# Constant products on TensorE in its waits ahead of the experts, and the last expert's rows placed by one-hot products

## The reference, cut to what matters

```python
logits = t @ w_router                       # 384 x 8
top_logit, top_e = top_k(logits, 2)
gates = softmax(top_logit)                  # two experts and two gates for each token
out[e] = (silu(x_e @ wg[e]) * (x_e @ wu[e])) @ wd[e]    # D_FF = 2816
y[token] = sum over its two experts of gate * out[row of this token]
x = x + mod_gate * y
```

## Time and profile before

| | us |
|---|---|
| median of three timed runs | 1924.35 |
| the profiled execution, its own time | 1944.56 |
| its span, first to last instruction | 1942.8 |
| TensorE busy in the span | 1843.7 |
| mean granted TensorE clock | 0.981 of full |

### The profile page before, as it was taken

The page is one execution under the profiler, slowest core; times in us unless marked ns, Lnnn a source line. Parts: engine busy times, 40 slices in busy tenths (PEclk is TensorE's granted clock), DMA queues, the critical chain, the costliest instruction groups (busy, mean ns, idle before and its releaser), DMA issues.

```text
span 1942.8 us, 31565 instructions
## 1 busy us (share of the span) xinstructions
PE 1843.7 (95%) x13609; PEld 1284.4 (66%) x13609; DVE 536.8 (28%) x1168; ACT 400.4 (21%) x901; POOL 125.2 (6%) x123
## 2 busy tenths in 40 slices
PE   6999999999999999999989999999998999999994
PEld 3554655879999887554785454568653456878783
DVE  2550336135555102165352000201111111111131
ACT  2221226110001001353222110311122121212120
POOL 0000111000000000000001001110010101020202
PEclk8999999999999999999999999999999999999997
DMA  8632237246542234133266556997689998999993
GB/s 311 236 132 87 87 109 260 86 140 206 175 152 76 96 126 177 51 134 134 80 244 216 200 195 204 392 383 251 228 278 394 384 364 301 365 344 359 345 383 126
DMA packets 234141, 427.93 MB, mean 220 GB/s; under 512 B 17694, under 2 KB 88701, under 8 KB 233678
## 3 DMA queue, kind: packets, MB, share of 16 engines
q1 hardware_dynamic: 218496, 411.65, 60.1%
q0 software_dynamic: 11360, 12.43, 1.9%
q10 hardware_dynamic: 4142, 1.72, 0.3%
HBM read 427.34 MB, written 29.00 MB: 235 GB/s over the span
## 4 chain that ended last, share of the span: by engine, by line
PE 88%; DMA 5%; DVE 3%; issue 2%; SPq 1%; ACT 1%; POOL 0%; POOLq 0%; DVEq 0%; ACTq 0%
PE bank L1099 24%; PE bank L588 11%; PE bank L824 10%; PE bank L1227 6%; PE bank L1192 6%; PE bank L876 6%; PE bank L635 4%; PE bank L1130 2%; PE bank L700 2%; PE bank L494 2%; DMA ring<-in_moe_w_gate_dram 2%; DMA ring<-in_w_mod_dram 1%; PE bank L919 1%; PE bank L908 1%; PE bank L552 1%
## 5 line engine op out<-in xcount | busy, mean ns | idle before, releaser
L1099 PE MATMUL bank<-ring,HTXN 128*32 128x384 f32 (+3 forms) x3104 | 287.6, 393 | 6.0 <-issue 3.9
L1318 ACT ACTIVATE arena<-bank 128x512 f32<-128x512 f32 (+3 forms) x317 | 140.8, 507 | 588.7 <-PE bank L824 178.6
L1099 PEld LDWEIGHTS bank<-ring,HTXN 128*32 128x32 f32 (+2 forms) x3104 | 202.9, 120 | 84.1 <-issue 61.1
L1099 PE MATMUL bank<-arena,HTXN 128*32 128x384 f32 (+3 forms) x2336 | 224.4, 394 | 2.6 <-issue 1.6
L1099 PEld LDWEIGHTS bank<-arena,HTXN 128*32 128x32 f32 (+2 forms) x2336 | 157.4, 122 | 63.3 <-issue 44.8
L2274 DVE TENSOR_TENSOR arena<-arena,bank 128x512 f32<-128x512 f32 x120 | 76.7, 683 | 414.3 <-PE bank L1099 385.2
L588 PE MATMUL bank<-ring,HTXN 128*128 128x512 f32 (+4 forms) x528 | 153.0, 452 | 1.0 <-DVE HTXN L2105 1.0
L1663 ACT ACTIVATE arena<-bank 128x512 f32<-128x512 f32 x120 | 65.0, 597 | 372.8 <-PE bank L1099 325.4
L588 PEld LDWEIGHTS bank<-ring,HTXN 128*128 128x128 f32 x528 | 96.2, 190 | 57.1 <-issue 47.2
L824 PE MATMUL bank<-HTXN,arena 128*128 128x192 f32 x704 | 121.4, 326 | 0.0
L876 PE MATMUL bank<-ring,arena 128*128 128x256 f32 x528 | 114.2, 379 | 2.6 <-DVE arena L2032 2.6
(11 more groups left out here) (349 smaller groups left out, 1849.0 us busy)
## 6 DMA issues: line engine op xcount, KB each, us to landing
ring<-in_moe_w_up_dram SPq DMA_DIRECT2D x53, 1024.0 KB
ring<-in_moe_w_gate_dram SPq DMA_DIRECT2D x49, 1024.0 KB
ring<-in_w_mod_dram SPq DMA_DIRECT2D x24, 2048.0 KB, 9.3
ring<-in_moe_w_down_dram SPq DMA_DIRECT2D x48, 1024.0 KB
arena<-in_moe_w_down_dram SPq DMA_DIRECT2D x40, 1024.0 KB
arena<-in_moe_w_gate_dram SPq DMA_DIRECT2D x39, 1024.0 KB
arena<-in_moe_w_up_dram SPq DMA_DIRECT2D x35, 1024.0 KB
ring<-in_w_in_dram SPq DMA_DIRECT2D x10, 2048.0 KB, 11.6
```

The source lines that it names most:

```text
L1099: last = mm(bank[row:row + rows_, col:col + cn], xe[:, i, k, at:at + rows_], wt[:, c0:c0 + cn], start=(k == 0 and col == 0), stop=(k == KT ...
L1318: return act_fn(out, in_, ACT.Copy)
```

## The change

Part one. A helper runs `n` products of the identity with 256 constant columns into a bank that the next real work overwrites. It is called in nine places directly ahead of a wait; in a tenth, twelve products with 128 columns go into unused columns of a bank. Where `fill` stood behind the wait it is moved ahead of it.

Part two. The last turn is kept to widths of up to 128 rows (its bodies for wider experts are gone), and if at least four experts other than expert 0 have more than 128 tokens, two places of the order are exchanged. The last turn writes nothing to DRAM. VectorE makes a table `slots` (token x row, holding the gate where the row is the token's), TensorE transposes it during the output products (`slot_tables`, at the fifth of eleven weight chunks), and after the drain of `yt` TensorE multiplies table by rows (`rows_to_tokens`) into six banks, which VectorE gates and adds to `X`. The late rows of the earlier experts are added during the last turn.

```diff
+            def keep_awake(bank, n):
+                for _ in range(n):
+                    mm(bank[:, 0:2 * P], ident, CST[:, 0:2 * P], start=True, stop=True)
-            def blocks(label, sources):
+            def blocks(label, sources, ready=None, n=0):
                 bank, full = fill(label)
+                if ready is not None:
+                    keep_awake(bank, n)
+                    pe.wait_ge(*ready)
...
-            mod_rows(0, 2)
+            mod_rows(0, 2, n=7)
             first_rows(0)
             mod_columns(0, 2)
+            begun = [fill(("xbc", m, "p")) for m in range(4)]
...
+            keep_awake(begun[0][0], 7)
             for t in range(NT):
                 pe.wait_ge(*drained(("nt", 0, t, 0)))
...
+                for _ in range(12 if j == 0 else 0):
+                    mm(begun[0][0][:, TOK:TOK + P], ident, CST[:, 0:P], start=False, stop=False)
                 for t in range(NT if j == 0 else 0):
                     pe.wait_ge(*drained(("nt", 0, t, 1)))
...
             to_feature_major(1)
+            first_plain = fill(("plain", 0))
+            keep_awake(first_plain[0], 5)
             ht_ready(1)
...
+                blocks(("qaT", t), [...], (qa_ready, t + 1), 5 if t == 0 else 0)
+                    blocks(("hT", i, q), [...], (kq_ready, i + 1) if q == 0 else None, 4 if last_k else 0)
+                blocks(("pT", n), [...], (pr_ready, n + 1), 3 if n == 3 else 0)
...
-            to_feature_major(3)
+            to_feature_major(3, 5)
+            bank, full = fill("lg_lanes")
+            keep_awake(bank, 3)
             ht_ready(3)
...
+            bank, full = fill("rank")
+            keep_awake(bank, 3)
             pe.wait_ge(sel_ready, 1)
...
+            def slot_tables(e, w):
+                pe.wait_ge(slots_ready, 1)
+                for n, label in enumerate(TABLES):
+                    bank, full = moe_fill(label, e)
+                    lanes = range(4) if n == 0 else [3] if w == 96 else []
...
+                    for t in range(NT):
+                        for lane in lanes:
+                            c = 32 * n if w == 96 and lane == 3 else 32 * lane % w
+                            last = mm(bank[32 * lane:32 * lane + 32, t * P:(t + 1) * P], slots[:, t, c:c + 32], ident,
+                                      start=(t == 0), stop=(t == NT - 1))
+                    last.then_inc(full, 1)
+            def rows_to_tokens(e, w):
+                for label in TABLES + [("y", 0, 0), ("y", 0, 1)]:
+                    pe.wait_ge(*moe_drained(label, e))
+                for t in range(NT):
+                    for h in range(2):
...
+                        elif w == 96 and h == 1:
+                            mm(PSUM[b][:, 0:256], table[0][0:96, :], rows_[0:96, 512:768], start=True, stop=False)
+                            for k in range(3):
+                                last = mm(PSUM[b][:, 256:512], table[k][96:P, :], rows_[96:P, 256 * k:256 * k + 256], ...)
+                        else:
+                            last = mm(PSUM[b][:, :], table[0][0:w, :], rows_[0:w, 512 * h:512 * h + 512], ...)
+                        last.then_inc(bank_full[b], 1)
...
-            then(v.tensor_scalar(tmp8, beaten, -2.0, float(2 * NE - 1), ALU.mult, ALU.add))
-            then(v.scalar_tensor_tensor(place_at, beaten, 2.0, tmp8, ALU.mult, ALU.min))
+            v.tensor_scalar(tmp8, ...); v.tensor_scalar(over_128[:, 1:8], cnt[:, 1:8], float(P), None, ALU.is_gt)
+            then(v.tensor_scalar(fourth, ...)); v.scalar_tensor_tensor(place_at, ...)
+            v.scalar_tensor_tensor(fourth, ...); then(v.tensor_reduce(over_128[:, 0:1], ...))
+            then(v.tensor_scalar(over_128[:, 0:1], ...)); then(v.scalar_tensor_tensor(place_at, ...))
...
+                if e == NE - 1:
+                    for t in range(NT):
+                        last = v.tensor_scalar(slots[:, t, :], iota, last_slot[:, t:t + 1], gl[:, t:t + 1], ALU.is_equal, ALU.mult)
+                    last.then_inc(slots_ready, 1)
...
+                else:
+                    moe_copy(TABLES[1], e, slot_t[:, 1, :], ...)
+                    for t in range(NT):
+                        dve.wait_ge(late_loaded[t], 16)
+                        add_rows(late_y, gl_before, t)
...
-            for t in range(NT):
-                dve.wait_ge(late_loaded[t], 32)
-                add_rows(late_y, gl, t)
+            for t in range(NT):
+                for h in range(2):
...
+                    dve.wait_ge(bank_full[b], n)
+                    then(v.tensor_tensor(late_y[:, t, at], PSUM[b][:, :], GB[:, 0 if t == 0 else 1, at], ALU.mult))
+                    v.tensor_tensor(X[:, t, at], X[:, t, at], late_y[:, t, at], ALU.add).then_inc(x_updated, 1)
```

More of the change, by code:

```diff
@@ L515, in ht_ready, with mod_rows @@
                     pe.wait_ge(*drained(("nt", n, t, 1)))
[L517 removed]
+            def mod_rows(layer, j, at=None, n=0):
                 label = ("mod", layer, j)
+                bank, full = fill(("mr", layer, j), at)
+                keep_awake(bank, n)
                 landed(label)
                 w = part(label, KT, 512)
[L523 removed]
                 for k in range(KT):
@@ L939, in _ @@
                         mod_grouped("mla", 1, j)
-                pe.wait_ge(kq_ready, i + 1)
+                last_k = i + 1 < len(TILES) and TILES[i + 1][0] == "k" and all(kind == "q" for kind, _ in TILES[i + 2:])
                 for q in range(2):
-                    blocks(("hT", i, q), [KQN[:, i % 2, 4 * q + k, :] for k in range(4)])
+                    blocks(("hT", i, q), [KQN[:, i % 2, 4 * q + k, :] for k in range(4)],
+                           (kq_ready, i + 1) if q == 0 else None, 4 if last_k else 0)
                 blocks(("hT", i, 2), [kq_v[:, i % 2, D + k * P:D + (k + 1) * P] for k in range(4)])
@@ L1198, in output_96 @@
                 return last
+            def slot_tables(e, w):
[3 more added lines that the diff above has]
+                    lanes = range(4) if n == 0 else [3] if w == 96 else []
+                    if not lanes:
+                        pe.sem_inc(full, 1)
+                        continue
+                    for t in range(NT):
[9 more added lines that the diff above has]
+                    for h in range(2):
+                        b, n = token_bank(t, h)
+                        pe.wait_ge(bank_free[b], n - 1)
+                        table = [slot_t[:, k, t * P:(t + 1) * P] for k in range(3)]
+                        rows_ = yt[:, 0, :]
+                        if w == 64:
+                            last = mm(PSUM[b][:, :], table[0][64 * h:64 * h + 64, :], rows_[64 * h:64 * h + 64, 0:512], start=True, stop=True)
+                        elif w == 96 and h == 1:
+                            mm(PSUM[b][:, 0:256], table[0][0:96, :], rows_[0:96, 512:768], start=True, stop=False)
+                            for k in range(3):
+                                last = mm(PSUM[b][:, 256:512], table[k][96:P, :], rows_[96:P, 256 * k:256 * k + 256], start=False, stop=(k == 2))
+                        else:
+                            last = mm(PSUM[b][:, :], table[0][0:w, :], rows_[0:w, 512 * h:512 * h + 512], start=True, stop=True)
+                        last.then_inc(bank_full[b], 1)
             def output(e, pieces):
@@ L1204, in output @@
                     if q == 2:
-                        for i in range(NPIECE):
+                        for i in range(NPIECE if e + 1 < NE else 1):
                             for h in range(2):
@@ L1270, in _ @@
             ORDER = [2, 1, 0, 3, 4, 5, 6]
-            BODIES = [(e, v) for e in range(NE) for v in ORDER]
+            LAST = NE - 1
+            BODIES = [(e, v) for e in range(NE) for v in ORDER if e < LAST or len(PIECES[v]) == 1]
             pe.br("experts")
@@ L1292, in go_to @@
                 likely = WIDTHS.index(LIKELY[e])
-                order = [likely] + [v for v in ORDER if v != likely]
+                order = [likely] + [v for v in ORDER if v != likely and (e, v) in BODIES]
                 for n, v in enumerate(order[:-1]):
```

87 lines of the change are left out of this document (57 added, 30 removed).

## The result

The changed kernel takes 1914.57 us (median of 8 runs, 1907.51 to 1929.02), the kernel before, on the same chip, 1924.61 (8 runs, 1921.73 to 1927.03). The ratio is 0.9948, 95% interval 0.9927 to 0.9968: 10.0 us faster. Forecast were 24.15 us and a time of 1900.2, with 1912 as the upper end; so the sign was right and less than half of the gain came.

A forecast was written before the change was run, and what follows sets the result against it. TensorE, busy 1843.7 of 1942.8 us, was taken to bound the kernel. Kept clock 17.45 and end less tables 9.5, minus route 0.9 and new falls 1.9, gave 24.15 us: 1924.35 to 1900.2, range 1892 to 1907.

The forecast's parts named there:

- stretches 1 to 3: Low-clock windows at the kernel's start (18.7, 28.9, 52.8); full clock there was to save 8.0 us.
- stretches 7, 8: Low-clock windows at 899.3 (attention) and 998.3; full clock was to save 3.0 and 0.7 us.
- falls that stay or come anew: Anywhere a wait stays open: one low-clock stretch charged at the mean, 1.9 us lost.
- route: VectorE's routing chain ahead of the experts' indices: six more chained operations, 0.9 us lost.
- tables: Last turn: 18 table products of 128 columns amid TensorE's output products, 3.0 us lost, bounds 2.0 to 4.0.
- the end: From last output product to last addition: 10.2 us at full clock instead of 22.7, 12.5 saved.
- rival C: Last products run at 1.2 GHz after the idle 0.8 us: 17.8 instead of 10.2 us, 1907.8 in all; chance 0.08.
- rival B: Products at all ten places run at the lower clock and outlast their waits: 7.7 us slower, 1932.1; chance 0.04.
- stretch 7: Low-clock window in attention (899.3), behind a 1.50 us wait three products were to fill; 3.0 us saved.
- A: At the filled waits, constant products don't hold the clock or only move low stretches: gain 8.6 us, 1915.8; chance 0.08.
- D: In the experts, the weight stream eats the gain won upstream; only the end's is left, 1914.9 us; chance 0.05.
- E: Blocks of 24 transposes count as idle; the clock falls at two places beside them, 1902.5 us; chance 0.08.

The follow-up runs named there:

- part one alone: Kernel before with all the constant products but its own old end; 1919.42 us, ratio 0.9957.
- filled end: Changed kernel plus two constant products in the pause between the last output product and the wait for the drained rows; 1904.78 us, ratio 0.9890.
- front with three: Changed kernel with three instead of seven constant products ahead of the second chunk of modulation weights; 1917.22 us, ratio 0.9952.
- transposes: Kernel with the filled end, each group of n constant products made into 4n transposes, the twelve narrow products kept; 1905.04 us, ratio 0.9887.
- best kernel: Kernel with the filled end, plus five products ahead of the dense block's hidden-rows wait and attention's three moved ahead of their bank's wait; 1902.02 us, ratio 0.9873.
- fill on part two alone: Kernel with only part two, plus two filling products in the pause behind the last output product; 1931.2 us, ratio 0.9939.
- hidden rows' wait filled: Kernel with the filled end, plus five constant products ahead of the wait for the dense block's last hidden tile; 1904.16 us, ratio 0.9879.
- part two alone: Changed kernel without any constant products, keeping the new end, tables and longer route chain; 1926.12 us, ratio 0.9995.
- the last experiment: The best kernel with three instead of seven constant products ahead of the first mod_rows; 1921.11 us, ratio 0.9884.

## Why the prediction was wrong

The steps in the order of its sum. Where a part is seen in a trace with fewer disturbances, I take it from there.

| term | forecast | measured | where |
|---|---|---|---|
| front, stretches 1 to 3 | -8.0 | -4.9 to -5.2 clock up late, -8.2 up early | changed kernel, part one alone; filled end |
| stretch 4 | -1.55 | -1.5 | all |
| stretches 5, 6 | -4.2 | -4.1 | all |
| the wait for a weight chunk behind them | none | 0 to +1.3 by the run, +0.8 in part one alone | all |
| stretches 7, 8 | -3.7 | -0.5 as written with a fall, -2.2 without one, -3.6 with the products in the wait | part one alone; front with three, transposes; best kernel |
| falls that stay or come anew | +1.9 | +3.4 (326 and 647), and others by run | part one alone |
| route | +0.9 | +0.7 | changed kernel against part one alone |
| tables | +3.0 | +2.0 | changed kernel against part one alone |
| waits for code in the last turn | none | +1.8, and -3.0 with the end filled | changed kernel; filled end |
| the end | -12.5 | -5.1 at the lower level, -11.3 held | changed kernel; filled end |

**The step that failed most is the end at full clock**, "10.2 us", and with it rival C, given 0.08. The mechanism was worked out right, and its length nearly: 17.8 forecast for the lower level, 17.66, 17.75 and 16.96 measured in three kernels, 11.5 in every one with the fill. That the 17.8 fits so closely is luck in part: the first tile's products began at full clock and took 3.66 us (1907.98 to 1911.64) instead of 5.2, and the second's took 5.71. What failed was the argument against it, that "the new pause is shorter than any that a fall followed" and the last products stood at full clock. The trace of before had pauses of 1.50 us and longer with a fall, and I took the shortest of them for a bound. Here 1.05 us was enough (priced at 0.8). The fill on part two alone shows that it isn't the falls ahead of the experts. Why so short a pause tips the clock here (behind it stand products of 96 and 32 rows instead of 128) was not separated. At full clock the end is 11.47 and not 10.2 because TensorE is not ahead of VectorE: a tile's products take 2.95 us (1888.17 to 1891.12), not 2.6 at most, the thin ones 0.26 a record and not 0.22. Cost of both: 7.4 us of the missing 14.1, of them 1.3 for the latter.

**The second is the overrun, rival B, at one place.** I had priced it at all ten places together. At the front it was real, 6.14 us of products in a wait of 3.56, since TensorE starts at the lower level; the "0.88 at the lower level" stood in the prediction and wasn't applied where the first `mod_rows` already showed 3.59 us. Cost: 2.9 us. At the other places the products were at full clock and fit, as forecast.

**The third is stretch 7.** The three products were costed as lying in the wait of 1.50 us. But `blocks` issues them behind `fill`, and `fill` itself waits for the bank's drain, which is the late one here (VectorE, `modT`). They came 1.42 us too late and added their own time. In part one alone and with the hidden rows' wait filled the clock fell there all the same (893.3); in three traces with the call at the same place (filled end, front with three, transposes) it didn't, and in two of these stretches 7 and 8 gave 2.2 us. "`fill`, moved ahead of the wait, takes banks that were drained long before" is the sentence that failed; it holds at the other places. Moved ahead of `fill`, they gave 3.6 with stretch 8, as forecast. Cost: 3.2 us with the fall, 1.5 without.

**The fourth is what comes anew.** One stretch was charged; two came in four of the nine traces with part one (326 and 647, which cost 1.7 us each), one of the two in three more, and others by the run. The profiled execution had one of 20.5 us behind the unfilled waits of 1.99 and 0.88 us: ahead of it the kernel was 7.4 us earlier than before, behind it level with it. In the one trace with the wait at 647 filled, another fall stood further on.

**What the sum had at nothing without a word** are the waits for code in the last turn. The one near its start grew from 2.03 to 4.62 us, the one at the up products shrank from 2.23 to 1.43: 1.8 us, and in the profiled run a low stretch of 6.8 us at the first of them besides. The wait at `L1072`, which was to grow to 1.8 us by the route, shrank from 0.90 to 0.16: TensorE now waits 2.23 us at `L1129` (1020.74) instead.

Against these, the tables cost 2.0 us and not 3.0, as much as the lower bound.

Part one alone gained 8.3 us and part two alone 1.0 by their ratios, together 9.3; the changed kernel gained 10.0 (interval 6.2 to 14.0). So there is no sign that one part hinders the other. A closer sum isn't to be had, since the low stretches differ from run to run by more than that: up to the first experts' product the changed kernel and the one with the filled end issue the same work, and their traces have it at 1020.74 and 1008.68.

Of the rivals, A fell (seven places of nine held, and part one alone has a ratio of 0.9957); D fell, by the last experiment's 16.5 and 17.6 us. E fell: the places beside blocks of transposes gave their 1.5 and 0.8 us, and transposes themselves filled as well as products did. The Trainium skill (TensorE: Matmul & The Clock Gate, Part 4: PE-mode transpose) says that transposes don't engage the full clock; the run with transposes as filling work at nine of the ten places and at the end (0.9887 against 0.9890) and its window at 1.00 disagree, and the measurement decides.

With the end, the attention place and the wait at 647 mended the kernel gains 24.5 us, for 24.15 forecast; that is luck in part, since the tables are cheaper, the held end is longer, and the 3.0 us from the waits for code were in no term.

## What to carry to other kernels

The shortest pause after which a trace shows a fall is no bound for a new pause: where new work starts behind a wait of about 1 us and itself runs with gaps, price it at the lower level, or fill the pause. A filling product works only if it stands ahead of every wait that can be the late one, the one for its own PSUM bank too; it is free only where the engine is at full clock already, so count it at twice its time at the start of a kernel. An unfilled wait of 1 us or more may or may not bring a fall: the same 1.42 us did in two traces here and didn't in three. Charge a share of them, and judge by several runs. And an edit that adds instructions can go with waits for code coming or going elsewhere in the program, of several us; look for waits put down to `issue` on both sides before a difference in time is put down to the edit.

## What the runs showed of the hardware

- Seven products of 128x256 in fp32 took 3.27 us at full clock and 6.14 at the start; in two traces of kernels that issue the same work up to there, the clock rose at 14.7 and at 22.6 us.
- Behind the waits of about 2 and 0.88 us ahead of attention, the clock fell for 20.5 us in the trace of the changed kernel and not at all in that of part one alone (2.45 and 0.88 us), until its next wait (893.3); both issue the same work up to there.
- The changed kernel's eight runs spread over 21.5 us with mean granted clocks of 0.986 to 0.997; span and clock multiplied give 1898 to 1902 us in all of them, so nearly all of the spread is time at the lower level. With the end filled, clocks are 0.997 to 0.998 and the spread of four runs is 6.5 us.
- 18 products of 128 columns with 32-column parts, amid output products without a gap, cost 2.0 us, 0.11 each.
- TensorE waited up to 4.6 us for nothing that the profile shows; each such wait of over 1 us within the experts ended 1.2 to 1.7 us behind the landing of a 16 KB transfer of instructions. Two more products elsewhere in the program went with one of 4.1 to 4.6 us being gone.
